# A hybrid decoder layer on one core: three changed orders, and a residual added by accumulating transfers

## The reference, cut to what matters

```python
mod = (silu(c) @ w_ada + b_ada)             # 6 blocks: shift, scale, gate twice
h = rmsnorm(x, norm_pre_mix) * (1 + sc1) + sh1
q, k, v, g, xr, gr = split(h @ w_in)
o, s_new = retention(rope(q), rope(k), v, s_ret)      # per sample: s_new = gamma^4 * s + k^T v
branch_ret = (groupnorm(o) * ret_gn_w * silu(g)) @ w_br_ret
hseq = rg_lru(causal_conv(xr)); branch_rnn = (hseq * gelu(gr)) @ w_br_rnn
ga, gb = split(sigmoid(h @ w_mgate + b_mgate))
x = x + g1 * rmsnorm((ga * branch_ret + gb * branch_rnn) @ w_out, norm_post_mix)
fg, fu = split((rmsnorm(x, norm_pre_ffn) * (1 + sc2) + sh2) @ w_ffn_in)
x = x + g2 * rmsnorm((silu(fg) * fu) @ w_ffn_out, norm_post_ffn)
```

## Time and profile before

| what | value |
|---|---|
| median of 3 runs | 1449.13 us (1448.87 to 1451.73) |
| the profiled execution's own time | 1449.33 us |
| its span, first to last instruction | 1447.5 us |
| mean granted PE clock | 0.979 |
| busy: PE, PEld, DVE, ACT, POOL | 95%, 89%, 50%, 33%, 13% |
| chain that ended last, by engine | PE 82%, DVE 9%, ACT 3%, DMA 3%, issue 2% |
| moved | 172.70 MB, mean 119 GB/s |

### The profile page before, as it was taken

The page is one execution under the profiler, slowest core; times in us unless marked ns, Lnnn a source line. Parts: engine busy times, 40 slices in busy tenths (PEclk is TensorE's granted clock), DMA queues, the critical chain, the costliest instruction groups (busy, mean ns, idle before and its releaser), DMA issues.

```text
span 1447.5 us, 23984 instructions
## 1 busy us (share of the span) xinstructions
PE 1377.7 (95%) x10324; PEld 1281.7 (89%) x10324; DVE 717.9 (50%) x998; ACT 484.3 (33%) x683; POOL 181.3 (13%) x284
## 2 busy tenths in 40 slices
PE   6699999899999899999999999999799999999995
PEld 3599999788997798799889879999799999999995
DVE  4349888522242475267437624966743333332225
ACT  4277778312231231232224123336422222212221
POOL 1013222000113212212320322000000000000000
PEclk8899999999999999999999999999899999999998
DMA  8422222475424434434442443243022222222321
GB/s 340 149 70 73 74 88 74 171 283 180 159 81 147 154 103 132 163 97 141 148 166 67 138 159 133 88 162 120 0 73 88 88 88 88 88 83 81 88 87 62
DMA packets 49930, 172.70 MB, mean 119 GB/s; under 512 B 5537, under 2 KB 7713, under 8 KB 49569
## 3 DMA queue, kind: packets, MB, share of 16 engines
q1 hardware_dynamic: 39456, 135.51, 28.1%
q0 software_dynamic: 9216, 33.56, 6.6%
q10 hardware_dynamic: 1152, 2.10, 0.4%
HBM read 149.82 MB, written 21.32 MB: 118 GB/s over the span
## 4 chain that ended last, share of the span: by engine, by line
PE 82%; DVE 9%; ACT 3%; DMA 3%; issue 2%; POOL 0%; SPq 0%; DVEq 0%; ACTq 0%; POOLq 0%
PE ps L760 66%; PE ps L769 3%; PE ps L1005 2%; PE ps L1016 2%; PE ps L808 1%; PE ps L988 1%; PE ps L1048 1%; PE ps L1034 1%; DMA raw<-in_w_brnn 1%; PE ps L891 1%; DMA raw<-in_w_out 1%; DVE w_lo L1517 1%; DMA raw<-in_w_rnn 1%; DVE x_res L1872 1%; DVE rsn L1867 1%
## 5 line engine op out<-in xcount | busy, mean ns | idle before, releaser
L760 PE MATMUL ps<-h_hi,w_hi 128*128 128x272 f32 x2096 | 444.1, 293 | 22.8 <-ACT xs L1287 9.5
L760 PE MATMUL ps<-h_hi,w_lo 128*128 128x272 f32 x2096 | 436.3, 290 | 0.0
L760 PE MATMUL ps<-h_lo,w_hi 128*128 128x272 f32 x2096 | 435.3, 289 | 0.0
L1517 DVE TENSOR_TENSOR w_lo<-raw,w_hi 128x1024 fp32r<-128x1024 f32 (+2 forms) x190 | 226.5, 1195 | 335.3 <-ACT w_hi L1189 332.9
L760 PEld LDWEIGHTS ps<-h_hi,w_hi 128*128 128x128 f32 x2096 | 333.9, 190 | 36.6 <-issue 18.0
L760 PEld LDWEIGHTS ps<-h_lo,w_hi 128*128 128x128 f32 x2096 | 332.4, 190 | 0.0
L760 PEld LDWEIGHTS ps<-h_hi,w_lo 128*128 128x128 f32 x2096 | 330.2, 190 | 0.0
L1189 ACT ACTIVATE w_hi<-raw 128x1024 fp32r<-128x1024 f32 (+2 forms) x190 | 195.6, 1030 | 355.9 <-PE ps L760 241.5
L1791 DVE SCALAR_TENSOR_TENSOR state<-state,ps 128x512 f32<-128x512 f32 x64 | 41.1, 684 | 111.1 <-PE ps L1048 110.9
L760 PE MATMUL ps<-a_hi,w_hi 128*128 128x272 f32 x308 | 63.8, 288 | 2.1 <-DVE a_lo L1526 2.1
L760 PE MATMUL ps<-a_hi,w_lo 128*128 128x272 f32 x308 | 63.8, 288 | 0.0
(11 more groups left out here) (238 smaller groups left out, 1848.8 us busy)
## 6 DMA issues: line engine op xcount, KB each, us to landing
raw<-in_w_head SPq DMA_DIRECT2D x48, 512.0 KB, 3.8
raw<-in_w_fin SPq DMA_DIRECT2D x38, 512.0 KB, 3.4
state<-in_state POOLq DMA_DIRECT2D x32, 512.0 KB, 4.1
out_rs<-state POOLq DMA_DIRECT2D x32, 512.0 KB, 3.9
raw<-in_w_rnn SPq DMA_DIRECT2D x24, 512.0 KB, 3.5
ada_more<-in_w_ada SPq DMA_DIRECT2D x23, 512.0 KB, 6.2
ada_raw<-in_w_ada SPq DMA_DIRECT2D x16, 512.0 KB, 14.6
raw<-in_w_bret SPq DMA_DIRECT2D x16, 512.0 KB, 3.5
```

The costliest lines, as they stand in the source:

```text
L760: mm = nc.tensor.matmul(dst[:, half, :], a, b[:, half * HALF:(half + 1) * HALF], start=first and j == 0, stop=last and j == 2)
L1517: V.tensor_tensor(lo[:, 0:cols], raw_slab(i)[0][:, 0:cols], hi[:, 0:cols].bitcast(F32), ALU.subtract).then_inc(lo_ready, 1)
```

## The change

There are four edits. SP issues the slabs of xr 1 and gr 1 right behind the 16 first slabs of `w_ada`, ahead of its wait for `h_ready`. In DVE's last turn of the recurrences one split of a later slab follows each of the first two recurrences, where before it followed the second and the third; the third recurrence then comes ahead of the remaining splits. POOL's load of state u + 2, with its wait for the store of state u - 2, moves from the start of step u to its end, behind the keys of u and the store of u - 1. And the second half of x after the first residual is stored to the output during the feed-forward block, between the first and the second slab of fo 0; at the end DVE only multiplies the second half's 8 tiles (all 272 columns each), and POOL adds them to the output in memory by four accumulating transfers of two k tiles (272 KB) each.

```diff
--- before.py
+++ after.py
@@ -536,6 +536,7 @@
         r_ready = sem("r_ready")
         mixed, mix_hi_ready, mix_ready, x1_ready = (sem(n) for n in ("mixed", "mix_hi_ready", "mix_ready", "x1_ready"))
         a_ready, y_done = sem("a_ready"), sem("y_done")
+        x1_stored, normed, y_added = sem("x1_stored"), sem("normed"), sem("y_added")
 
         def vcol(name, i, n=1):
             a = VEC[name][0] + i
@@ -706,6 +707,7 @@
                 if n == KD:
                     load_to(pl.slab[("gr", 0, "w", 0)])
                 sp.dma_start(ada_raw[:, n, :], w["w_ada"][n // KD, n % KD]).then_inc(ada_in[n], 16)
+            load_to(pl.slab[("gr", 1, "w", 0)])
             sp.wait_ge(h_ready, KD)
             sp.wait_ge(c4_ready, 1)
             sp.dma_start(rg_w[:], w["w_rg"]).then_inc(rg_in, 16)
@@ -735,12 +737,14 @@
             sp.wait_ge(mix_ready, KD)
             states_stored(sp)
             sp.dma_start(xr_[:], w["x"]).then_inc(xres_in, 16)
+            load_to(pl.slab[("fo", 0, "w", 0)])
+            sp.wait_ge(h_ready, 3 * KD)
+            sp.dma_start(out["y"][:, :, cols_of(1)], xr_[:, :, cols_of(1)]).then_inc(x1_stored, 16)
             load_to(len(pl.slabs) - 1)
-            for half in range(2):
-                for k in range(KD):
-                    sp.wait_ge(y_done, KD * half + k + 1)
-                    sp.dma_start(out["y"][:, k, cols_of(half)], xr_[:, k, cols_of(half)]).then_inc(stored, 16)
-            sp.wait_ge(stored, 16 * (1 + 2 * KD))
+            for k in range(KD):
+                sp.wait_ge(y_done, k + 1)
+                sp.dma_start(out["y"][:, k, cols_of(0)], xr_[:, k, cols_of(0)]).then_inc(stored, 16)
+            sp.wait_ge(stored, 16 * (1 + KD))
 
 
         @block.tensor
@@ -1645,15 +1649,15 @@
                 ahead(("xr", n))
                 conv(n)
                 ahead(("gr", n))
-                for i in recurrences_at(n):
+                gate_slabs = list(GATE_TILES.get(n, ()))
+                last_turns = recurrences_at(n) + (recurrences_at(NR) if n == NR - 1 else ())
+                for i in last_turns:
                     decays(i)
                     recur(i)
-                for m in GATE_TILES.get(n, ()):
+                    if n == NR - 1 and i < NR - 1:
+                        ahead(("gb", gate_slabs.pop(0)))
+                for m in gate_slabs:
                     ahead(("gb", m))
-                    if n == NR - 1 and m == GATE_TILES[n][0]:
-                        for i in recurrences_at(NR):
-                            decays(i)
-                            recur(i)
             for m in range(KD):
                 split_to(pl.slab[("bn", m, "w", 1)] + AHEAD)
                 wait_took(dve, ("gb", m))
@@ -1958,9 +1962,10 @@
                     add_to_norm(first + KD + 1, KD - 1, cols_of(1), norm_summed)
             wait_took(dve, ("fo", KD - 1))
             one_over("post2", 1)
-            samples_normed(gate2)
+            do(V.tensor_tensor(all_samples(mo), all_samples(mo), for_samples(gate2), ALU.mult))
             for k in range(KD):
-                add_normed(1, k, y_done)
+                y = mo[:, k, cols_of(1)]
+                do(V.tensor_tensor(y, y, rsn[:, cols_of(1)], ALU.mult), normed, wait=False)
 
 
         @block.gpsimd
@@ -2049,10 +2054,6 @@
                 wait_freed(pool, ("tks", h))
                 for b in range(NB):
                     u = h * NB + b
-                    if STATES <= u + 2 < H * NB:
-                        last = u + 2 - STATES
-                        pool.wait_ge(s_stored[last % STATES], 16 * (last // STATES + 1))
-                        load_state(u + 2)
                     if u >= 2:
                         hh, bb_ = divmod(u - 2, NB)
                         wait_full(pool, ("sn", hh, bb_, 1))
@@ -2065,10 +2066,20 @@
                                        ALU.subtract), kst_ready)
                     if u:
                         store_state(u - 1)
+                    if STATES <= u + 2 < H * NB:
+                        last = u + 2 - STATES
+                        pool.wait_ge(s_stored[last % STATES], 16 * (last // STATES + 1))
+                        load_state(u + 2)
             store_state(H * NB - 1)
 
 
             states_stored(pool)
+            pool.wait_ge(x1_stored, 16)
+            for k in range(0, KD, 2):
+                pool.wait_ge(normed, k + 2)
+                pool.dma_start(out["y"][:, k:k + 2, cols_of(1)], mo[:, k:k + 2, cols_of(1)], accum_op=ALU.add)\
+                    .then_inc(y_added, 16)
+            pool.wait_ge(y_added, 16 * (KD // 2))
 
 
 def constants():
```

## The result

| | median us | range | ratio to before | 95% interval |
|---|---|---|---|---|
| before, in the same comparison | 1449.56 | 1448.87 to 1451.73 | | |
| after | 1470.21 | 1467.34 to 1471.15 | 1.0137 | 1.0118 to 1.0155 |

The changed kernel is slower by 20.6 us, and the prediction (1440.4, range 1435 to 1445) is wrong in size and in sign. The profiled execution took 1470.91 us with a span of 1469.1 and a mean granted clock of 0.972, against 1447.5 and 0.979 before.

What follows compares the result with a forecast made beforehand. PE, busy 95% of the span, was taken as the bound, so only shortening its work or filling its holes counts. Terms: 11.3 - 0.7 - 2.0 + 0.3 = 8.9 us off 1449.33, giving 1440.4, range 1435 to 1445.

Steps and rivals of the forecast that it cites:

- The front: At xr 1, early slabs close PE's 9.46 us hole and avoid the lower clock behind it: 11.3 us gained.
- The recurrences: From gb 6 to bn 1, PE's lead becomes a 6.4 us hole at a queued slab, lower clock behind: 0.7 lost.
- The keys: In the heads, earlier keys gain 3.7 us, later state loads cost 5.7 in heads two to four: 2.0 lost.
- Rival 3: In the heads, back-to-back state loads and stores take 6.1 us each, six waits cost 13.2: 1447.9 us, chance 0.06.
- the gain of 3.7: In the first head, keys come 2.6 us earlier and the clock holds, 1.1 more: 3.7 us gained.
- The end: In the tail, DVE only multiplies and four accumulating transfers take 3.8 us each: 0.3 us gained.
- Rival 5: In the tail, accumulating transfers run one behind another, 24 us in all: 1457.3 us, chance 0.03.

Runs made afterwards that it cites:

- a_only: Kernel before with the first edit alone, slabs issued ahead of SP's wait for h_ready; 1439.33 us, ratio 0.9931.
- ab_only: Kernel before with the first two edits alone, early slabs and DVE's reordered splits; 1439.56 us, ratio 0.9933.
- ab_look: Kernel before with the first two edits, state load between keys and store, and SyncE looking 7 instead of 13 w_ada slabs ahead; 1430.56 us.
- a_look: ab_look without the second edit (DVE's reordered splits); 1433.52 us, ratio 0.9877.
- load_first: Changed kernel with the load of state u + 2 right behind the keys, ahead of the store and its wait for DVE's update; 1440.67 us.
- ab_look_5: The kernel of ab_look again, in five rounds beside the same kernel without the second edit; 1429.22 us, ratio 0.9856.
- load_freed: Changed kernel with the state load still behind the keys and DVE's update of state u - 1, but ahead of the store; 1453.92 us.

## Why the prediction was wrong, point by point

**The front: right.** Predicted 11.3, measured 11.0 at 92 us (the recurrent gates, L891 before, start at 81.26 against 92.23) and 11.0 in the medians of `a_only`. The hole and the lower clock behind it went, and nothing came in their place.

**The recurrences: right in mechanism, and in size within what can be told.** Predicted 0.7 lost by a hole of 6.4 us with a low clock behind; the changed kernel has 4.99 us with a first pair of 0.82, and lost 1.1 from 218 to 374. In the medians `ab_only` against `a_only` makes it 0.2. Less the 11.0 of the front, bn 0 starts at 273.8 and PE resumes at 297.5, as forecast (273.8 and 297.4). What was missed is the wait of 2.44 us ahead of bn 0: behind it the granted clock is 0.61 and then 0.71 until 268, so 1.6 of the 5.2 us of lead were gone before the hole came. The prediction had taken from one hole of 2.11 us that the clock holds behind such a length. That the slab comes when the queue has worked down to it was only argued; `ab_look` and `a_look` bear it out, since a shorter queue removes the hole with and without the second edit. The rule of the Trainium skill (the page "DMA: Bandwidth & Descriptors", "Queues, rings and completion order") that an engine takes a queue's descriptors in ring order agrees with this, and with p3 above, where the second of a pair pays; at p1, with a slab of SP's queue in between, the order changed nothing (6.4 us either way). What the prediction did not draw from this is that the cure is one number away.

**The keys: the step that failed.** The term "A transfer of a state takes 4.0 us ..., and the store issued at that very time took 5.0, so it lands at 565.1 to 566.1" put the load of the changed kernel at the duration of transfers that had POOL's queue to themselves. The earlier trace rows is a median over loads (4.1 us by themselves), which before were issued after the store ahead had landed, and stores (3.9), and the earlier trace rows a store with nothing ahead of it on that queue. The change makes each load the second of a pair. For p3 the prediction also says "only the store is beside it", which its own trace contradicts: SP issues a slab between 604.9 and 606, where the load was to go out at 604.9.

```profile
raw<-in_w_head SPq DMA_DIRECT2D x1, 512.0 KB, 3.7
```

In the changed kernel it goes out 0.6 us behind the load. Measured 5.9 to 7.1 us, so the six waits are 1.94 to 3.15 us each, 15.2 in sum, where the prediction had 5.7 and an upper bound of 7.2. Rival 3 had the right mechanism (back to back, 6.1 us, 13.2 us of waits) and a chance of 0.06.

A second step in the same part failed, and it is the larger: the clock behind new waits was costed in the recurrences, and put at nothing here. Its waits of 0.7 and 1.2 us, shorter than the one of 2.11, may have allowed that; the measured ones did not. Behind the waits at p3 it adds over 3 us per head, 10.8 in all (26.0 less 15.2), where the longer waits add 9.5 to the 5.7 forecast. Rival 3 left it out too, and would have come to 1458.7 with it. (By its own 6.1 us its waits sum to 13.6 and not 13.2.)

A third: "In the first head p3 would wait up to 0.5 us ... The other p units have over 1 us of room." Its waits were 0.98 at p2 and 2.61 at p3, for loads of 7.04 and 6.52 us, and they ate the gain of 3.7 whole. Even with loads in time the next keys stand behind a load that waits for a store, and the gain varies: 0.7 us in the profiled execution of `load_first`, where PE waits 3.20 for keys, 5.5 in that of `ab_look_5`, where it waits 0.97. Why that wait differs so is open.

**The end: the second term that failed.** Predicted 3.8 us per accumulating transfer and 0.3 gained, bounds 1.0 gained and 3 lost; measured 4.8, 6.0, 6.7 and 7.5 us and 4.2 lost, beyond the bound. (That bound does not follow from its own words: twice the 1.7 us of a plain store would land at 1446.4, before the old end.) The reason given for the 3.8, half the bytes of a state but a read as well, priced bytes; the runs show 1088 packets where the plain transfer has 320, and 2.7 times the engines' time. Rival 5 asked for succession; they overlap, but keep the engines at 0.9 or more of their time in most of those slices. That the early store of x is hidden was right. The estimate from the Trainium skill ("DMA: Bandwidth & Descriptors", latency of the first byte, 1 us against 600 ns) would have had the last land at 1445.1, 2.1 us after its issue; the trace disagrees, as it took 7.5.

**The sum.** 11.0 gained in the front, 1.1 lost in the recurrences, nothing gained in the first head, 26.0 lost in the others, 1.2 lost from there to the last norm, 4.2 in the tail: 21.5 lost, the 21.6 of the two spans. Against the forecast of 8.9 gained that is 30.5 us, of which 20.3 are the waits for states and the clock behind them, 4.5 the tail, and 3.7 the first head.

## What to carry to other kernels

Take a transfer's duration from a row where it has the neighbours, on its queue and on the others, that the change gives it; a median over transfers with the queue to themselves was too low here by 2 to 3 us. When a load is moved behind a store, both its later issue and its place behind count, and each new wait of PE costs its own length and what the granted clock loses behind it (here 15.2 us of waits and 10.8 behind them). Where a lead ends at the same transfer each time, shorten what is queued ahead of that transfer before moving more work forward.

## What the runs showed of the hardware that was not expected

An accumulating transfer of 272 KB landed 6.5 us after its issue where the same one without accumulation took 3.0, and the four of them kept the 16 engines 2.7 times as long for the same bytes; two of them beside SP's stores of 136 KB raised the last four of these from 1.7 to 4.1 us. A load of 512 KB issued less than 1 us behind a store took 4.8 to 7.7 us in the changed kernel, and one issued less than 1 us ahead of a store 4.5 to 6.4 in `load_freed`, against a median of 4.1 for the loads before. And waits of PE of 2.4 to 3.2 us were followed by the lower clock in some places (2.44 us ahead of bn 0, 2.36 at p3 of head 3) and not in others (2.80 at p1 of head 2).
